# Key and query norms of a DeltaNet layer: sums of squares over partitions as matmuls of two parts in the matmul format

## The reference

```python
def l2_normalize(x):
    return x * lax.rsqrt(jnp.sum(jnp.square(x), axis=-1, keepdims=True) + NORM_EPS)

def gdn_mixer(x, S0, conv_buf, w_in, conv_w, a_log, dt_bias, norm_w, w_out, chunked):
    proj = x @ w_in
    qkv = proj[..., :GDN_CONV_CH]
    ...
    qkv_c, new_buf = causal_dwconv(qkv, conv_buf, conv_w)
    qkv_c = jax.nn.silu(qkv_c.astype(f32))
    q = qkv_c[..., :GDN_QK_W].reshape(bsz, t, GDN_HEADS, GDN_DK)
    k = qkv_c[..., GDN_QK_W:2 * GDN_QK_W].reshape(bsz, t, GDN_HEADS, GDN_DK)
    ...
    q = l2_normalize(q) * (GDN_DK ** -0.5)
    k = l2_normalize(k)
    ...
```

## Time and profile before

| what | value |
|---|---|
| median of 3 runs | 1519.74 us (1518.29 to 1522.4) |
| the profiled execution | 1519.67 us |
| its span in the trace | 1517.7 us |
| granted clock of TensorE, mean | 0.997 |
| TensorE busy | 1496.4 us, 99% |
| VectorE busy | 1264.8 us, 83% |
| ScalarE (ACT) busy | 1028.3 us, 68% |
| HBM, mean over the span | 310 GB/s |

### The profile page before, as it was taken

The page is one execution under the profiler, slowest core; times in us unless marked ns, Lnnn a source line. Parts: engine busy times, 40 slices in busy tenths (PEclk is TensorE's granted clock), DMA queues, the critical chain, the costliest instruction groups (busy, mean ns, idle before and its releaser), DMA issues.

```text
span 1517.7 us, 24271 instructions
## 1 busy us (share of the span) xinstructions
PE 1496.4 (99%) x9242; PEld 1307.5 (86%) x9242; DVE 1264.8 (83%) x1334; ACT 1028.3 (68%) x974; POOL 118.4 (8%) x177
## 2 busy tenths in 40 slices
PE   9999999999999999999999999999999999999997
PEld 8989999999999988888888888888888888888875
DVE  6897557886368779999899899889889889889896
ACT  5884447664344457777777778778778778777773
POOL 4303000120030130000000000000000000003100
PEclk9999999999999999999999999999999999999999
DMA  9968036896565559999999999999999999999991
GB/s 294 348 214 268 7 102 214 285 318 206 171 195 175 165 180 398 396 360 394 388 377 389 388 365 384 378 386 384 384 378 373 385 375 380 385 388 376 392 414 63
DMA packets 226795, 471.29 MB, mean 311 GB/s; under 512 B 10164, under 2 KB 69668, under 8 KB 226425
## 3 DMA queue, kind: packets, MB, share of 16 engines
q1 hardware_dynamic: 215704, 433.56, 78.4%
q0 software_dynamic: 11024, 36.78, 7.2%
HBM read 448.75 MB, written 21.79 MB: 310 GB/s over the span
## 4 chain that ended last, share of the span: by engine, by line
PE 93%; DVE 3%; ACT 2%; issue 1%; DMA 1%; SPq 0%; DVEq 0%; ACTq 0%
PE bank L2320 13%; PE bank L2324 13%; PE bank L2321 13%; PE bank L2350 13%; PE bank L418 13%; PE bank L2356 6%; PE bank L424 6%; PE bank L2183 3%; PE bank L2188 1%; PE bank L2332 1%; DVE low L380 1%; DMA wab<-in_gdn_w_in_dram 1%; PE bank L2028 1%; PE bank L2015 1%; ACT high L375 1%
## 5 line engine op out<-in xcount | busy, mean ns | idle before, releaser
L380 DVE TENSOR_TENSOR low<-raw,high 128x2048 fp32r<-128x2048 f32 x404 | 921.4, 2294 | 135.2 <-ACT high L375 132.4
L375 ACT ACTIVATE high<-raw 128x2048 fp32r<-128x2048 f32 x404 | 773.1, 1917 | 286.4 <-PE bank L2324 89.1
L2320 PE MATMUL bank<-high,xgh 128*128 128x512 f32 x896 | 353.4, 394 | 0.0
L2321 PE MATMUL bank<-high,xgl 128*128 128x512 f32 x896 | 349.4, 390 | 0.0
L2324 PE MATMUL bank<-low,xgh 128*128 128x512 f32 x896 | 240.2, 390 | 0.4 <-DVE low L380 0.4
L2324 PEld LDWEIGHTS bank<-low,xgh 128*128 128x128 f32 x896 | 168.0, 188 | 36.5 <-DVE low L380 1.1
L2321 PEld LDWEIGHTS bank<-high,xgl 128*128 128x128 f32 x896 | 168.4, 188 | 33.9
L2320 PEld LDWEIGHTS bank<-high,xgh 128*128 128x128 f32 x896 | 168.3, 188 | 33.6
L418 PE MATMUL bank<-xhb,high 128*128 128x266 f32 (+1 forms) x816 | 168.8, 288 | 1.8 <-DVE utail L1218 1.7
L418 PE MATMUL bank<-xlb,high 128*128 128x266 f32 (+1 forms) x816 | 166.8, 286 | 0.0
L2350 PE MATMUL bank<-high,hth 128*128 128x512 f32 x448 | 139.8, 393 | 0.0
(11 more groups left out here) (464 smaller groups left out, 1389.8 us busy)
## 6 DMA issues: line engine op xcount, KB each, us to landing
raw<-in_moe_w_gu_dram SPq DMA_DIRECT2D x224, 1024.0 KB, 7.0
raw<-in_moe_w_down_dram SPq DMA_DIRECT2D x112, 1024.0 KB, 7.1
raw<-in_ffn_w_gu_dram SPq DMA_DIRECT2D x22, 1024.0 KB, 5.4
raw<-in_gdn_w_in_dram SPq DMA_DIRECT2D x16, 1024.0 KB, 11.6
raw<-in_sc_w_in_dram SPq DMA_DIRECT2D x12, 1024.0 KB, 4.9
raw<-in_ffn_w_down_dram SPq DMA_DIRECT2D x11, 1024.0 KB, 5.7
tok<-zeros POOLq DMA_DIRECT2D x26, 384.0 KB, 12.1
s<-in_state_gdn_S_dram POOLq DMA_DIRECT2D x8, 512.0 KB, 5.0
```

What stands on the lines that cost most here:

```text
L375: eng.activation(high[:, n % SPLIT, :], raw[:, n % RAW, :], ACT.Copy).then_inc(high_ready, 1)
L380: eng.tensor_tensor(low[:, n % RAW, :], raw[:, n % RAW, :], high[:, n % SPLIT, :].bitcast(F32), ALU.subtract).then_inc(low_ready, 1)
L2320: pe.matmul(out, xgh[:, 4 * kh + k, :], wh[:, k, :], start=kh + k == 0, stop=False)
L2321: pe.matmul(out, xgl[:, 4 * kh + k, :], wh[:, k, :], start=False, stop=False)
```

## The change

Each square x is written as h + l, h the value rounded to the matmul format and l the rest, and the sum is ones times h plus ones times l, accumulated in the bank.

- ACT makes a copy of the ones in the format once, before group 0 (`ones_r`). After each of the four squares it copies the squares into the format (`square_h`, in a place of its own). Before the square of groups 1 to 3 it waits for VectorE's subtraction of the group before (`sq_ready`).
- VectorE subtracts h from the squares, in place (`square_l`), in its rounds 3, 5, 8 and 9, behind the split of the weight of that round.
- TensorE waits for this subtraction instead of the square. It makes four matmuls of 512 columns in the format where two in FP32 stood. Their places in its program are the same.
- The sum of the sample's squares stays as it is; its wait counts on, since `sq_ready` now counts nine steps instead of five.

```diff
+        square_l = place("square_l", [128, 8, NP], F32R, at=region + 4 * QT * N)
+        square_h = place("square_h", [128, 8, NP], F32R, at=a_at)
+        ones_r = place("ones_r", [128, 128], F32R, at=layer0_end)
...
+        def group_halves(g):
+
+            return square_h[:, 4 - 4 * (g % 2):8 - 4 * (g % 2), :], square_l[:, 4 * (g % 2):4 * (g % 2) + 4, :]
...
                     if g >= 2:
                         act.wait_ge(qk_ready, g - 1)
-                    act.activation(group(g), qkv[:, 4 * g:4 * g + 4, 0:NP], ACT.Square).then_inc(sq_ready, 1)
+                    if g:
+                        act.wait_ge(sq_ready, 2 * g)
+                    else:
+                        step(act.activation(ones_r[:, :], ones[:, :], ACT.Copy))
+                    step(act.activation(group(g), qkv[:, 4 * g:4 * g + 4, 0:NP], ACT.Square))
+                    step.wait()
+                    act.activation(group_halves(g)[0], group(g), ACT.Copy).then_inc(sq_ready, 1)
...
                 if n < OUT0 - 1:
                     split_low(dve, n + SPLIT)
+                if n in (3, 5, 8, 9):
+                    g = (3, 5, 8, 9).index(n)
+                    dve.wait_ge(sq_ready, 2 * g + 1)
+                    dve.tensor_tensor(group_halves(g)[1], group(g), group_halves(g)[0].bitcast(F32), ALU.subtract).then_inc(sq_ready, 1)
...
             def square_sums(g):
 
-                pe.wait_ge(sq_ready, g + 1)
+                pe.wait_ge(sq_ready, 2 * g + 2 if g < 3 else 9)
...
                 for i in range(2):
-                    pe.matmul(bank[4 + 2 * (g % 2) + i][:, :], ones[:, :], group(g)[:, 2 * i:2 * i + 2, :].rearrange("p t i -> p (t i)"),
-                              start=True, stop=True).then_inc(sq_psum, 1)
+                    for p, w in enumerate(group_halves(g)):
+                        last = pe.matmul(bank[4 + 2 * (g % 2) + i][:, :], ones_r[:, :],
+                                         w[:, 2 * i:2 * i + 2, :].rearrange("p t i -> p (t i)"), start=p == 0, stop=p == 1)
+                    last.then_inc(sq_psum, 1)
...
-                    pe.wait_ge(sq_ready, 5)
+                    pe.wait_ge(sq_ready, 9)
```

## The result

| | before | after |
|---|---|---|
| median, 5 runs each | 1519.74 us (1517.89 to 1522.4) | 1545.57 us (1543.19 to 1547.13) |
| ratio, 95% interval | | 1.0161 [1.0146, 1.0175] |
| span of the profiled execution | 1517.7 us | 1542.5 us |
| granted clock, mean over the span | 0.997 | 0.987 |
| from ACT's square of group 0 to the first decode matmul | 58.7 us | 84.1 us |

The change makes the kernel 25.8 us slower, 1.6%. The last two lines say where: all of it lies in the stage of the input projection, and what follows is the same length. The forecast was 1540, the range ended at 1545; the median lies 0.6 above its end.

What follows compares the result with a forecast made beforehand. TensorE, busy 99% of the span, was taken as the bound. 1519.7 us plus 15.4 for the waits (savings and vanished old waits counted) plus 4.8 for the clock gave 1539.9, so 1540 us; range 1534 to 1545.

Steps and rivals of the forecast that it cites:

- What bounds the kernel, and that nothing takes a loss back: Whole span: TensorE, 99% busy, is the bound; no later wait on memory is long enough to swallow a gain or loss.
- The saving of 0.8 a group: TensorE's sums: four matmuls in the format cost 0.9 us instead of 1.7 a group, 3.2 us saved over four groups.
- The four waits: TensorE waits for VectorE's subtraction behind slot 4, inside slots 6 and 9, behind slot 9: 4.2, 3.2, 6.8, 7.2 us.
- place 0: Behind weight tile (slot) 4: the subtraction ends at 53.2, TensorE waits 4.2 us, saves 0.8 and is 3.4 late.
- The old waits: TensorE's 1.7 us before slot 9 all but gone; 0.37 before the sample's sum and 0.82 before the decode matmuls vanish.
- place 3: Behind slot 9: the subtraction stands behind the convolution of slot 9's own output; TensorE waits 7.2 us, is 16.6 late.
- The clock: Behind the waits of 4.2, 6.8 and 7.2 us TensorE's clock falls to 1.2 GHz: 3 x 1.6 = 4.8 us.
- The harmless wait: Between full slots, 1.7 us idle left the clock at 1.00; so no fall was counted for the wait of 3.2.
- Rival 2: All four waits and more drop the clock, or later small matmuls fall too: 1541.5 to 1543.1, up to 1545; chance 0.2.
- Rival 1: The waits come but the clock holds: 1519.7 + 15.4 = 1535.1 us; chance 0.13.
- that the low halves are in time: VectorE's subtractions end before TensorE asks, only the saving is left: 1516.5 us; chance 0.02, with its half-way house 0.04.
- that the format isn't faster: The sums' new matmuls take 1.72 us a group as before: 3.2 us more, 1543; chance 0.03.

Runs made afterwards that it cites:

- the filled kernel: The changed kernel, with TensorE making matmuls whose results are overwritten while it would wait at the four places; 1534.60 us, ratio 1.0094 to the kernel before.

## Why the prediction was right, and where not

**What bounds the kernel, and that nothing takes a loss back.** Right: the rest of the span is 1414.4 us after 1415.2.

**The saving of 0.8 a group.** Right at full rate (the sums in the filled kernel start 0.23 us apart), and out of reach in the change itself, where half rate makes them 2.08.

**The four waits.** 4.2, 3.2, 6.8 and 7.2 were worked out, 4.17, 3.34, 6.89 and 7.26 came. The subtraction of place 0 ends at 53.16 (53.2 forecast). The old waits vanished as said. Without the clock 15.4 was forecast; the filled kernel, which is that case, gave 14.0 by the medians and 16.2 in its stage. That ACT would be ready just in time at place 3 is right too: in the filled kernel it had 0.44 us to spare.

**The clock: the step that failed, by size.** I took three falls at 1.6 us, 4.8. There were four, and they cost 10.4 us by the rows, 9 to 12 by the filled kernel. The 5.6 us between 10.4 and 4.8 are the whole of what the forecast is short by (25.8 against 20.2). Two signs that I had named lie outside their bounds for the same reason: convolution 9 began 16.8 us later than before, not 9 to 14, and the decode matmuls came at 128.08, not at 118 to 124. Two things were wrong in the term for the clock.
- The price. One fall was read from the only stretch of the trace before that showed one, and taken as a fixed sum. It was a fall behind 0.79 us of idle time, with 3.4 us at half rate. In the change, behind waits of 3 to 7 us, the clock fell in the middle of the wait and stayed low for 4.4 to 5.7 us of work once it had begun again, 2.2 to 2.8 us lost for each. Where the waits were cut to 2.4, a fall cost 1.6 to 1.7. The stretches at half rate in this stage were 3.4, 6.8 or 10.2 us long, and only what lies behind the end of the wait costs.
- The harmless wait. From 1.7 us without a fall I argued that a wait of 3.2 might pass. It may (the kernel with ACT's wait loosened shows one), but it is no threshold: behind 1.75 and 1.84 the clock fell in two of the profiled executions, behind 2.35 and 2.36 it didn't. (Nor did it behind 1.72 to 1.80 in four others, and it did behind 2.32, 2.37, 2.38 and 2.45.) Whether it falls depends on more than the length.

Rival 2 (four falls, 1541.5 to 1543.1, up to 1545 with long ones) had the mechanism, with 0.2; the median lies above even its 1545. Rival 1, that the clock holds, is refuted by the four falls. The sentence on the Trainium skill, page "TensorE: Matmul & The Clock Gate", section "Loop structure matters more than you think", can be judged now: its example of 8 us is not contradicted. No wait here was that long, but waits of 6.9 and 7.3 brought the clock down in each of the four profiled executions that had them whole. The example taken for the long waits alone would have given less than was measured (18.6 against 25.8), since the shorter ones brought it down as well.

**The other rivals.** That the low halves are in time is refuted by the waits; that the format isn't faster is refuted by the filled kernel.

**What I hadn't weighed.** The added work is not free even where nothing waits for it: with all four subtractions in time the kernel is where it was, not 3.2 us faster, since VectorE then is on the chain all the way. And the needless wait of ACT, hidden in the change, costs some 4 us as soon as its cover is gone.

## What to carry to other kernels

When a result gets one more step on another engine, look up what stands ahead of that step in that engine's order, and whether any of it waits for the consumer itself: behind slot 9, TensorE waited for VectorE, which waited for TensorE's slot 9, whatever the step's own 1.2 us. Price a wait of TensorE as its length plus what the clock takes afterwards; here that was half as much again, and filling the waits with matmuls that nobody reads gave it back. A matmul that gets cheaper is worth little where the chain runs over two other engines as well: the 3.2 us saved came to 1.3 when nothing else was added, which is not to be told from nothing.

## What the runs showed of the hardware

- Four waits of 2.32 to 2.37 us between like work: two brought the granted clock down, two didn't. The shortest in the profiled executions that did so was 1.75 us between full slots.
- After a wait of 7.26 us TensorE worked for 5.7 us at half rate, after 6.89 for 4.4. The clock can fall while TensorE waits (2.5 us into the wait of 4.17) or after it has begun again (0.7 us after the wait of 2.32).
- A GpSimd tensor-tensor of 128x1024, itself 2.4 to 2.9 us, stretched a VectorE tensor-tensor of 128x2048 from 2.28 to 6.33 and to 4.06 us, and one of 3.45 us in the kernel before stretched one to 4.88; VectorE's multiply-adds out of the banks beside another one kept their 2.68. Why the one suffers and the other not, these runs don't show.
